# Experts' rows weighted at their eviction and added into DRAM by an accumulating scatter, instead of gathered and summed at the end

## The reference

```python
logits = xt @ w_router + b_router                 # 512 x 32
top_val, top_idx = lax.top_k(logits, 4)
gates = softmax(top_val)
# per expert e, for the tokens that chose it:
hu = x_e @ w_up_gate[e] + b_up_gate[e]
g, u = min(hu[:, :1024], 7), clip(hu[:, 1024:], -7, 7)
y = (g * sigmoid(1.702 * g) * (u + 1)) @ w_down[e] + b_down[e]
moe[t] = sum_k gates[t, k] * y[t, k]              # 1024 wide
out = rms_norm(h + moe, final_norm_gain)
```

## Time and profile before

| | |
|---|---|
| device time, 3 runs | 1854.43, 1854.58, 1856.55 us (median 1854.58) |
| profiled execution: its time, its span | 1854.94 us, 1853.1 us |
| mean granted PE clock | 0.977 |
| busy: PE, DVE, ACT, POOL | 95%, 77%, 62%, 17% |
| share of the chain that ended last | PE 91%, DVE 3%, DMA 2% |
| DMA: moved, mean rate | 480.54 MB, 259 GB/s |

### The profile page before, as it was taken

How to read it: one execution, slowest core, us unless ns; L and a number is a source line. 1 busy time by engine, 2 the same in 40 slices (tenths; PEclk the granted TensorE clock), 3 DMA queues, 4 the chain that set the end, 5 groups by cost and what they waited for, 6 DMA issues and landing times.

```text
span 1853.1 us, 26498 instructions
## 1 busy us (share of the span) xinstructions
PE 1760.0 (95%) x8935; PEld 1291.2 (70%) x8935; DVE 1435.9 (77%) x1480; ACT 1140.8 (62%) x1118; POOL 317.6 (17%) x241
## 2 busy tenths in 40 slices
PE   6999999999989889999999999999999999999980
PEld 5777777777768657777777777777777777777750
DVE  4566576567656689888988988888898888889855
ACT  4544453455352457777777777777777777777741
POOL 0112201210115012112111211211121121111001
PEclk9999999999989889999999999999999999999995
DMA  7321222122116479999999999999999999999935
GB/s 200 86 75 46 68 79 79 45 68 79 53 73 211 160 253 380 383 369 367 353 371 376 349 367 376 367 356 368 367 363 362 377 361 360 369 375 355 361 140 227
DMA packets 158097, 480.54 MB, mean 259 GB/s; under 512 B 12740, under 2 KB 82676, under 8 KB 125072
## 3 DMA queue, kind: packets, MB, share of 16 engines
q1 hardware_dynamic: 150816, 463.08, 68.6%
q0 software_dynamic: 7248, 17.04, 2.7%
HBM read 471.04 MB, written 16.78 MB: 263 GB/s over the span
## 4 chain that ended last, share of the span: by engine, by line
PE 91%; DVE 3%; DMA 2%; POOL 1%; issue 1%; ACT 1%; SPq 0%; POOLq 0%; DVEq 0%; ACTq 0%
PE psum L284 27%; PE psum L285 26%; PE psum L286 26%; PE psum L881 1%; PE psum L625 1%; PE psum L655 1%; PE psum L641 1%; PE psum L902 1%; PE psum L608 1%; PE psum L865 1%; DVE acc L1779 1%; PE psum L911 1%; PE psum L592 1%; PE psum L602 1%; POOL braw L1875 1%
## 5 line engine op out<-in xcount | busy, mean ns | idle before, releaser
L1513 DVE TENSOR_TENSOR wL<-wraw,wH 128x2048 fp32r<-128x2048 f32 x388 | 884.0, 2289 | 135.3 <-ACT wH L381 135.2
L381 ACT ACTIVATE wH<-wraw 128x2048 fp32r<-128x2048 f32 x388 | 744.2, 1919 | 312.3 <-PE psum L286 294.1
L284 PE MATMUL psum<-wH,xTH 128*96 128x512 f32 x1040 | 419.1, 403 | 8.0 <-DVE wL L1513 4.5
L285 PE MATMUL psum<-wL,xTH 128*96 128x512 f32 x1040 | 410.5, 395 | 0.0
L286 PE MATMUL psum<-wH,xTL 128*96 128x512 f32 x1040 | 410.1, 394 | 0.0
L284 PEld LDWEIGHTS psum<-wH,xTH 128*96 128x96 f32 x1040 | 169.3, 163 | 80.7 <-DVE wL L1513 5.2
L286 PEld LDWEIGHTS psum<-wH,xTL 128*96 128x96 f32 x1040 | 169.2, 163 | 72.9 <-issue 0.2
L285 PEld LDWEIGHTS psum<-wL,xTH 128*96 128x96 f32 x1040 | 169.5, 163 | 69.6
L284 PE MATMUL psum<-wH,aTH 128*96 128x512 f32 x496 | 201.0, 405 | 0.0
L285 PE MATMUL psum<-wL,aTH 128*96 128x512 f32 x496 | 195.4, 394 | 0.0
L286 PE MATMUL psum<-wH,aTL 128*96 128x512 f32 x496 | 194.9, 393 | 0.0
(11 more groups left out here) (247 smaller groups left out, 2177.3 us busy)
## 6 DMA issues: line engine op xcount, KB each, us to landing
wraw<-in_w_up_gate SPq DMA_DIRECT2D x256, 1024.0 KB, 6.9
wraw<-in_w_down SPq DMA_DIRECT2D x128, 1024.0 KB, 7.3
fraw<-in_w_in SPq DMA_DIRECT2D x68, 512.0 KB, 3.9
yk<-yd SPq DMA_DIRECT2D x16, 512.0 KB, 9.7
wraw<-in_w_out SPq DMA_DIRECT2D x4, 1024.0 KB, 6.1
xt<-in_x SPq DMA_DIRECT2D x4, 512.0 KB, 5.4
hres<-in_x SPq DMA_DIRECT2D x4, 512.0 KB, 5.0
x2d<-xr SPq DMA_DIRECT2D x4, 512.0 KB, 4.2
```

The lines of the kernel that those rows point to most:

```text
L284: nc.tensor.matmul(ps, lh, rh, start=start, stop=False)
L285: nc.tensor.matmul(ps, lh, rl, start=False, stop=False)
L381: nc.scalar.activation(wH[:, b % SPLIT, :], raw(b), ACT.Copy).then_inc(p_hi, 1)
L1513: V.tensor_tensor(wL[:, b % SPLIT, :], raw(b), wH[:, b % SPLIT, :].bitcast(F32), ALU.subtract).then_inc(p_lo, 1)
```

## The change

The choices are no longer stored apart and summed at the end.
- `sums` in DRAM (640 rows of 1024) starts as a copy of `hres`: SP issues five stores of 512 KB before expert 1's weights. Rows 512 to 639 are there for unused slots, one per partition.
- `gate_of` in DRAM has the 2048 gates in order token, choice; SP stores it from SBUF after expert 1's loads, as 128 x 4 runs of 4 words.
- The assignment number is now token x 4 + choice; the token is a shift of it, and a third DVE operation limits it to the partition's own spare row.
- Per block POOL copies indices again (`ixq`) and fetches 96 gates of 4 B into `gs` by an indirect load.
- ACT's eviction waits for `gs_in` and multiplies by `gs`; the scatter goes to `sums` with an add, all 96 rows of it.
- The end loads four tiles of `sums`; ACT squares and roots them, DVE takes the reciprocal and writes the final tile, SP stores it. POOL has no part in it, and each tile has its own buffer.

```diff
@@ constants and DRAM
-    c[:, K_AS:K_TH] = k * T + j * P + s + 1
+    c[:, K_AS:K_TH] = (j * P + s) * TOPK + k + 1
+    c[:, K_DR] = T + np.arange(P)
-    yd = nc.dram_tensor("yd", [TOPK * T, D], F32, kind="Internal").ap()
+    sums = nc.dram_tensor("sums", [T + P, D], F32, kind="Internal").ap()
+    gate_of = nc.dram_tensor("gate_of", [T * TOPK, 1], F32, kind="Internal").ap()
@@ SP
+            def start_sums(j):
+                sp.wait_ge(h_ready, 2 * j + 2)
+                sp.dma_start(sums[j * P:(j + 1) * P, :], hres[:, j, :]).then_inc(sums_out, 16)
+                if j == 0:
+                    sp.dma_start(sums[T:T + P, :], hres[:, j, :]).then_inc(sums_out, 16)
             rows_out(3)
+            for j in range(NT):
+                start_sums(j)
             load_body(1)
             sp.wait_ge(over_ready, 1)
+            sp.dma_start(gate_of.rearrange("(j p k) o -> p j (k o)", p=P, k=TOPK), gates[:, :, :]).then_inc(gate_out, 16)
             sp.dma_start(over_list[:, :], ovi[:, 0:1]).then_inc(over_out, 16)
...
             for j in range(NT):
-                for k in range(TOPK):
-                    r = k * T + j * P
-                    sp.dma_start(yk[:, j, k, :], yd[r:r + P, :]).then_inc(yk_in[j - 1] if 0 < j < NT - 1 else yk_edge[min(j, 1) * TOPK + k], 16)
+                sp.dma_start(acc[:, j, :], sums[j * P:(j + 1) * P, :]).then_inc(acc_in[j], 16)
@@ ACT
+                act.wait_ge(gs_in, 16 * i + 16)
-                A(ysb[0:BLK, :], ybank[0:BLK, :], ACT.Copy).then_inc(y_ready, 1)
+                A(ysb[0:BLK, :], ybank[0:BLK, :], ACT.Copy, scale=gs[0:BLK, 0:1]).then_inc(y_ready, 1)
@@ DVE
-            V.tensor_scalar(tab[:, :, 0], tab[:, :, 1], NONE | (T - 1), None, ALU.bitwise_and).then_inc(tab_ready, 1)
+            V.tensor_scalar(tab[:, :, 0], tab[:, :, 1], TOPK.bit_length() - 1, None, ALU.logical_shift_right).then_inc(tab_ready, 1)
+            dve.wait_ge(tab_ready, 2)
+            V.tensor_scalar(tab[:, :, 0], tab[:, :, 0], cst[:, K_DR:K_DR + 1], None, ALU.min).then_inc(tab_ready, 1)
@@ POOL
+            def fetch_gates(i, code):
...
+                if not first(i):
+                    gp.wait_ge(y_ready, n)
+                    gp.wait_ge(gs_in, landed)
+                G.tensor_copy(ixq[:, :], src).then_inc(ixq_ready, 1)
+                gp.wait_ge(gate_out, 16)
+                gp.wait_ge(ixq_ready, after)
+                gp.indirect_dma_start(gs[0:BLK, :], None, gate_of, bass.IndirectOffsetOnAxis(ap=ixq[0:BLK, 1:2], axis=0),
+                                      bounds_check=last_assignment, oob_is_err=False).then_inc(gs_in, 16)
@@ scatter
-                gp.indirect_dma_start(yd, bass.IndirectOffsetOnAxis(ap=ixs[0:BLK, 1:2], axis=0), ysb[0:BLK, :], None,
-                                      bounds_check=last_assignment, oob_is_err=False).then_inc(y_out, 16)
+                gp.indirect_dma_start(sums, bass.IndirectOffsetOnAxis(ap=ixs[0:BLK, 0:1], axis=0), ysb[0:BLK, :], None,
+                                      bounds_check=last_sum, oob_is_err=True, compute_op=ALU.add).then_inc(y_out, 16)
+            gp.wait_ge(sums_out, 16 * (NT + 1))
+            fetch_gates(0, 0)
             scatter(0, 0)
             with gp.Fori(2, NE - 2) as i:
                 gather(i + 2, NBC * (i + 2))
+                fetch_gates(i - 1, NBC * (i - 1))
                 scatter(i - 1, NBC * (i - 1))
```

More of the change, by code:

```diff
@@ L67 @@
 C_GB = C_GA + D
-K_ID, K_TF, K_TB, K_KF, K_KB, K_REL, K_SL, K_IO, K_LT, K_ON, K_CD, K_P1, K_EPS, K_SE, K_AS, K_TH, K_END = np.cumsum(
-    [0, P, P, P, T, T, 3 * P, QH, NE * NBC, P, P, NE * (NB - 1), 1, 1, NE, NT * TOPK, NB - 1]).tolist()
+K_ID, K_TF, K_TB, K_KF, K_KB, K_REL, K_SL, K_IO, K_LT, K_ON, K_CD, K_P1, K_EPS, K_SE, K_AS, K_TH, K_DR, K_END = np.cumsum(
+    [0, P, P, P, T, T, 3 * P, QH, NE * NBC, P, P, NE * (NB - 1), 1, 1, NE, NT * TOPK, NB - 1, 1]).tolist()
 R_LF, R_LB, R_NG, R_FG, R_END = 0, 16, 32, 40, 48
@@ L97, in constants @@
     j, k = np.arange(NT * TOPK) // TOPK, np.arange(NT * TOPK) % TOPK
-    c[:, K_AS:K_TH] = k * T + j * P + s + 1
-    c[:, K_TH:K_END] = BLK * np.arange(1, NB)
+    c[:, K_AS:K_TH] = (j * P + s) * TOPK + k + 1
+    c[:, K_TH:K_DR] = BLK * np.arange(1, NB)
+    c[:, K_DR] = T + np.arange(P)
     return c
@@ L197, in build @@
     ixs = sb("ixs", [P, 2], I32)
+    ixq = sb("ixq", [P, 2], I32)
+    gs = sb("gs", [P, 1])
     gates = sb("gates", [P, NT, TOPK])
@@ L263, in build @@
     at[0] = small_top
-    yk = sb("yk", [P, NT, TOPK, D])
-    acc = sb("acc", [P, 2, D])
-    fin = sb("fin", [P, 2, D])
+    acc = sb("acc", [P, NT, D])
+    fin = sb("fin", [P, NT, D])
     nc_psum = nc.alloc_psum_tensor("psum", [P, 8 * 512], F32)
@@ L520, in _ @@
             for j in range(NT):
-                for k in range(TOPK):
-                    r = k * T + j * P
-                    sp.dma_start(yk[:, j, k, :], yd[r:r + P, :]).then_inc(yk_in[j - 1] if 0 < j < NT - 1 else yk_edge[min(j, 1) * TOPK + k], 16)
+                sp.dma_start(acc[:, j, :], sums[j * P:(j + 1) * P, :]).then_inc(acc_in[j], 16)
             for j in range(NT):
[L525 to L532, removed]
+                sp.wait_ge(fin_ready, j + 1)
+                sp.dma_start(out[0, j * P:(j + 1) * P, :], fin[:, j, :]).then_inc(out_done, 16)
+            sp.wait_ge(out_done, 16 * NT)
+            for s_, n_ in ((x2_out[0], 32), (x2_out[1], 32), (over_out, 16), (sums_out, 16 * (NT + 1)), (gate_out, 16)):
                 sp.wait_ge(s_, n_)
@@ L1257, in _ @@
             for j in range(NT):
[L1258 to L1261, removed]
+                act.wait_ge(acc_in[j], 16)
+                A(fin[:, j, :], acc[:, j, :], ACT.Square, accum_out=stat[:, 32 + j:33 + j]).then_inc(sq2, 1)
                 act.wait_ge(sq2, j + 1)
                 A(stat[:, 40 + j:41 + j], stat[:, 32 + j:33 + j], ACT.Sqrt, scale=1.0 / D, bias=eps).then_inc(sd2, 1)
-                if j < NT - 1:
-                    act.wait_ge(rs2, j + 1)
-                    A(fin[:, j % 2, :], acc[:, j % 2, :], ACT.Copy, scale=stat[:, 44 + j:45 + j]).then_inc(fs_ready, 1)
         @block.vector
@@ L1766, in _ @@
             run_overflow(dve, overflow, needs_code=True)
[L1769 to L1782, removed]
+            dve.wait_ge(wr_in, 64)
+            for j in range(NT):
                 dve.wait_ge(sd2, j + 1)
                 V.reciprocal(stat[:, 44 + j:45 + j], stat[:, 40 + j:41 + j]).then_inc(rs2, 1)
-                if j < NT - 1:
-                    return
                 dve.wait_ge(rs2, j + 1)
-                dve.wait_ge(wr_in, 64)
-                V.scalar_tensor_tensor(out=fin[:, j % 2, :], in0=acc[:, j % 2, :], scalar=stat[:, 44 + j:45 + j], in1=fgain[:, :],
+                dve.wait_ge(acc_in[j], 16)
+                V.scalar_tensor_tensor(out=fin[:, j, :], in0=acc[:, j, :], scalar=stat[:, 44 + j:45 + j], in1=fgain[:, :],
                                        op0=ALU.mult, op1=ALU.mult).then_inc(fin_ready, 1)
[L1792 to L1796, removed]
         @block.gpsimd
@@ L1884, in _ @@
             G.memset(xg[:, :], 0.0).then_inc(xg_zero, 1)
+            G.memset(gs[:, :], 0.0).then_inc(gs_zero, 1)
             gp.wait_ge(xg_zero, 1)
-            gp.wait_ge(tab_ready, 2)
+            gp.wait_ge(tab_ready, 3)
             gp.wait_ge(x2_out[0], 32)
             gp.wait_ge(x2_out[1], 32)
-            last_token, last_assignment = gp.to_reg(T - 1), gp.to_reg(TOPK * T - 1)
+            last_token, last_assignment, last_sum = gp.to_reg(T - 1), gp.to_reg(TOPK * T - 1), gp.to_reg(T + P - 1)
             def gather(i, code):
@@ L1902, in gather @@
                                       bounds_check=last_token, oob_is_err=False).then_inc(xg_in, 16)
+            def fetch_gates(i, code):
+                src = tab[:, code, :] if isinstance(code, int) else tab[:, bass.ds(code, 1), :].rearrange("p o c -> p (o c)")
+                landed, n = (16 * i, i) if isinstance(i, int) else (gp.to_reg(16 * i), gp.to_reg(i))
+                after = i + 1 if isinstance(i, int) else gp.to_reg(i + 1)
+                gp.wait_ge(gate_out, 16)
+                gp.wait_ge(gs_zero, 1)
+                if not first(i):
+                    gp.wait_ge(y_ready, n)
+                    gp.wait_ge(gs_in, landed)
+                G.tensor_copy(ixq[:, :], src).then_inc(ixq_ready, 1)
+                gp.wait_ge(gate_out, 16)
+                gp.wait_ge(ixq_ready, after)
+                gp.indirect_dma_start(gs[0:BLK, :], None, gate_of, bass.IndirectOffsetOnAxis(ap=ixq[0:BLK, 1:2], axis=0),
+                                      bounds_check=last_assignment, oob_is_err=False).then_inc(gs_in, 16)
             def scatter(i, code):
@@ L1922, in _ @@
                 gather(i + 2, NBC * (i + 2))
+                fetch_gates(i - 1, NBC * (i - 1))
                 scatter(i - 1, NBC * (i - 1))
             for i in range(NE - 3, NE):
+                fetch_gates(i, NBC * i)
                 scatter(i, NBC * i)
@@ L1930, in overflow @@
```

(1 more changed line is left out.)

9 lines of the change are left out of this document (5 added, 4 removed).

## The result

| | before | after |
|---|---|---|
| median of 4 runs | 1855.57 us (1854.43 to 1858.45) | 1951.26 us (1945.66 to 1956.05) |
| profiled execution, span | 1854.94, 1853.1 | 1949.97, 1948.2 |
| mean granted PE clock | 0.977 | 0.959 |
| PE busy | 1760.0 us (95%) | 1793.5 us (92%) |
| POOL busy | 317.6 us (17%) | 609.8 us (31%) |

The ratio is 1.051 (95% interval 1.048 to 1.054). The change makes the kernel 5% slower; 1830 us was forecast. The end came as forecast, the expert loop did not.

The account below looks back on a forecast made before the run. PE was taken to bound the expert loop, with the last 51.3 us exposed. 1854.94 - 27.6 + 0.3 + 2.2 = 1829.8 us, 1829.5 at the median, stated as 1830; range 1825 to 1858 us.

Parts of the forecast that it names:

- The end: After the last eviction: fewer loads and no POOL work end the span at 1825.5 instead of 1853.1, gain 27.6 us.
- The step that failed: Expert loop, POOL behind the gather: copy, 0.78 us gap and issue put the gate fetch out by 1064.7.
- Landing: Expert loop: fetched gates land at most 7.3 or 6.5 us after the issue ends, between 1067 and 1072.
- The slack: Expert loop: ACT's eviction may be 5.3 us late before PE stands; even gates at 1072 cost 0.
- Rival 3: Expert loop: gates come more than 5.3 us late in every expert; 1 us beyond the slack costs +30, 1860; chance 0.09.
- The scatter's add: At the end: the last scatter, now adding 96 rows, lands 2.0 us later than its 3.61 us.
- The part behind the last square: At the end: from the last square to the end of the span, 7.7 us instead of 8.33.
- Before the loop: Ahead of the expert loop: one more DVE operation on the code table costs +0.3 us; five stores are hidden, cost 0.
- Traffic: Expert loop: the adding scatter's extra 1.3 or 2.2 us of transfer fit into 3.7 us spare, cost 0.
- rival 2: Expert loop: the adding scatter makes DMA the bound, 1.7 us per expert, +51, 1881; chance 0.14.
- The gate list: Near the start: storing 2048 gates as 512 runs takes 5.4 us of transfer, less 3.2 slack: 2.2 us.
- Rival 1: Near the start: the list of gates costs by the run, 18.4 us instead of 2.2, total 1846; chance 0.27.

## Why the prediction was wrong

- **The step that failed:** "so I expect the fetch issued by 1064.7", and with it the cost 0 of the added wait. I priced the issue on a row beside splits (3.52 us), but the copy ahead of it, "then a copy", at next to nothing: the gather's own copies take 0.7 us (22.7 us in 31). Behind the gather it falls into the run of splits and takes 5.63 us; then 0.78 us of gap and 2.29 us of issue: 1060.7 + 8.7 = 1069.4, as the fetch without its wait shows. The earlier trace rows showed the three splits back to back from 1061.50; the copy had to be laid beside them.
- **Landing.** Forecast: at most 6.5 to 7.3 us after the issue's end. Used 4.6 us after it in a short turn (1072.0 to 1076.6) and 6.3 us after it in a long one (1113.3 to 1119.7). That part was safe: the gates are late by POOL, not by DMA.
- **The slack was right, and not enough.** 5.3 us; 5.04 late costs nothing, 6.04 late costs PE 0.66, 12.21 late costs 6.83. Rival 3, at 0.09, has the mechanism ("gates more than 5.3 us late"), but I barred it with the speed of 96 words and not with POOL, and its price of 1 us per expert was much too low: 123.6 us over the 28 late evictions are 4.4 each.
- **What I had not thought of** is the feedback. I treated the slack as free: up to 5.3 us late, cost 0. But a late eviction moves work on ACT and DVE together, DVE loses the pauses in which POOL gets its turn, and the next fetch is late by 12 us. The kernel whose eviction does not wait has no gather above 3.52 us; the kernel after has a long one in every second turn. Late by less than the slack is not the same as in time.
- **The clock** was in no term: 34.0 us of the 123.6 are PE at the lower level at its gaps.
- **The end was right.** Forecast -27.6, measured -29.4. The scatter's add +1.8 (taken 2.0), squares 1.4 to 1.9 apart (forecast 1.45), the final operations 1.28 us (forecast 1.28). The part behind the last square is 6.05 us, not 7.7: from the end of the last DVE operation to the end of the span it is 3.05 us instead of 4.7, and I had left that as it was. Before the loop I forecast +0.3 us; the first eviction comes 0.8 us later.
- **Traffic was right at 0**, and rival 2 is out: 96 added rows per expert at 368 GB/s leave PE busy throughout, at a price per row under its 0.71 us.
- **The gate list**: 2.2 us forecast; at most 1.3 us of transfer, nothing of PE. Rival 1 is out: the 512 runs did not each pay what a word of the other list did.
- Without the failed step the sum of 1829.5 us is near what the kernel with the fetch elsewhere gives, 1829.09. That it fits to 0.4 us is partly luck: against the kernel before on the same chip the gain is 27.9 us where 25.1 was forecast, and the terms behind it differ: the end is 1.8 us better in the kernel after, and the 2.2 us for the gate list did not come.

## What to carry to other kernels

Lay each added POOL instruction, the tiny copies too, beside what DVE does in the same microseconds: the ones that take 0.2 to 1.0 us where DVE leaves room took up to 14.5 us beside its splits here. Fetch a small operand a whole turn ahead, where it costs the same instructions and no wait. And when a new wait uses up most of a slack, ask what the engines do while they catch up, since that sets whether the next turn is as late as this one or later.

## What the runs showed of the hardware

**How long DVE can hold POOL.** The Trainium skill (SBUF — State Buffer, Who interferes with whom, and for the waiting Summary: rules for kernel authors) says that a DVE instruction with two inputs in SBUF contends with a GpSimd instruction that reads SBUF, and that the one that starts later waits until the first is finished. The splits have two such inputs, the copies and the indirect issues read a table of indices; and 3.52 us against 1.00 is about one split longer. But in the kernel whose fetch is not awaited that issue's row begins at 1057.22, 0.36 us ahead of the split:

```profile
1057.58 2.28 DVE L1518 TENSOR_TENSOR wL<-wraw,wH 128x2048 fp32r<-128x2048 f32 x1
```

The split took its usual 2.28 us, and the issue still ended (1060.74) 0.9 us behind the split's end at 1059.86. And 5.63 and 14.53 us are longer than any one DVE instruction: they span several. In both the trace goes beyond the rule, unless the issue reads its table later than its row begins, which no row here shows. The issue of 14.53 us ended 0.9 us after DVE's first idle moment:

```profile
1101.46 6.68 DVE L1517 TENSOR_TENSOR wL<-wraw,wH 128x2048 fp32r<-128x2048 f32 x3
1108.07 0.21 DVE L1608 TENSOR_SCALAR sel<-cst 96x128 bf16 x1
1108.20 2.28 DVE L1517 TENSOR_TENSOR wL<-wraw,wH 128x2048 fp32r<-128x2048 f32 x1
```

1108.20 + 2.28 = 1110.48, and the issue ended at 1111.37. There DVE has run out of splits because ACT stands at the eviction, which waits for the gates behind this very issue. All 14 long issues of the kernel after end 0.9 us behind such a moment. So does the one of the scatter that overwrites, where the eviction waits for nothing, DVE has worked from 720.15 on, and the issue ends at 751.92:

```profile
748.78 2.28 DVE L1517 TENSOR_TENSOR wL<-wraw,wH 128x2048 fp32r<-128x2048 f32 x1
751.63 2.29 DVE L1517 TENSOR_TENSOR wL<-wraw,wH 128x2048 fp32r<-128x2048 f32 x1 [0.57 <-ACT wH L385]
```

So POOL does not always get its turn between two DVE instructions. What decides whether it does stays open: from 1096.84 on, DVE's instructions follow one another as in the short turn, where the issue was through after 3.52 us; one thing that differs is that DVE had made no pause for 17 us before (from 1079.58). That the missing pause is what makes the issue long is read from these rows; no run put a pause into a turn behind a late eviction.

**Adding in the scatter** cost 1.5 us from the start of the issue to POOL's `done` for 96 rows of 4 KB with little other traffic, 0.5 us of it in the issue, and was not to be seen in the loop (one run of each kind).

**Small stores**: by the estimate above 128 words of 4 B took away 5.1 us of all 16 engines' transfer time, 512 runs of 16 B beside them at most 1.3 us more. Why the second list is so much cheaper stays open.
